# Two-block transformer kernel: VectorE's convolution taps dealt out 3 / 2 / 4 per weight piece instead of 3 throughout

## What is computed

```python
def conformer_conv_branch(a_glu, gate, dw, dw_b, ln_g, ln_b, w_proj):
    a, b = jnp.split(a_glu, 2, axis=-1)
    u = a * jax.nn.sigmoid(b)
    u = lax.conv_general_dilated(
        u, dw[:, None, :], window_strides=(1,), padding=[(CONV_K - 1, 0)],
        dimension_numbers=("NWC", "WIO", "NWC"), feature_group_count=CONV_CH) + dw_b
    u = layer_norm(u, ln_g, ln_b)
...
    return u @ w_proj
```

## Time and profile before

| what | value |
|---|---|
| median of 3 runs | 1293.46 us (1291.17 to 1294.85) |
| the profiled execution, its own time | 1293.89 us |
| its span, first to last instruction | 1292.2 us |
| PE busy | 1134.4 us (88%) |
| DVE busy | 964.9 us (75%) |
| POOL busy | 579.2 us (45%) |
| ACT busy | 567.3 us (44%) |
| mean granted TensorE clock | 0.978 of full speed |

### The profile page before, as it was taken

The page is one execution under the profiler, slowest core; times in us unless marked ns, Lnnn a source line. Parts: engine busy times, 40 slices in busy tenths (PEclk is TensorE's granted clock), DMA queues, the critical chain, the costliest instruction groups (busy, mean ns, idle before and its releaser), DMA issues.

```text
span 1292.2 us, 15750 instructions
## 1 busy us (share of the span) xinstructions
PE 1134.4 (88%) x5652; PEld 785.7 (61%) x5652; DVE 964.9 (75%) x1944; ACT 567.3 (44%) x1036; POOL 579.2 (45%) x576
## 2 busy tenths in 40 slices
PE   6999899999999997999679887798878987777787
PEld 6989798899999996977436332363323632222222
DVE  5589989974578765686798877977679777777554
ACT  5476767664345444695522323413224232222211
POOL 0099999999940000000344544444444444444331
PEclk9999999999999998999889999899998999999999
DMA  7644443444555555535599999999999999999996
GB/s 263 203 132 163 130 131 128 133 135 159 171 193 169 186 163 164 198 103 180 185 421 423 428 427 426 407 426 427 428 426 394 426 427 426 427 426 427 424 428 255
DMA packets 127647, 374.37 MB, mean 290 GB/s; under 512 B 6864, under 2 KB 82640, under 8 KB 94672
## 3 DMA queue, kind: packets, MB, share of 16 engines
q0 software_dynamic: 36864, 268.45, 49.5%
q1 hardware_dynamic: 88496, 100.67, 23.8%
q10 hardware_dynamic: 2208, 4.24, 1.0%
HBM read 372.29 MB, written 1.05 MB: 289 GB/s over the span
## 4 chain that ended last, share of the span: by engine, by line
PE 52%; DMA 23%; DVE 15%; ACT 5%; issue 4%; POOL 0%; SPq 0%; DVEq 0%; POOLq 0%
DMA big<-in_experts,big 17%; PE unit L729 12%; PE unit L418 11%; PE unit L420 11%; PE unit L419 11%; DMA row<-in_experts,big 3%; DVE work L1843 3%; DMA conv_in<-in_experts,big 2%; DVE w_lo L1430 2%; DVE big L1762 1%; DVE conv_acc L1453 1%; ACT L837 1%; DVE big L1759 1%; ACT probs L1178 1%; DVE big L1855 1%
## 5 line engine op out<-in xcount | busy, mean ns | idle before, releaser
L418 PE MATMUL unit<-in_hi,w_hi 128*128 128x256 f32 x1184 | 359.1, 303 | 3.1 <-DVE in_lo L1517 3.1
L419 PE MATMUL unit<-in_lo,w_hi 128*128 128x256 f32 x1184 | 336.2, 284 | 0.0
L420 PE MATMUL unit<-in_hi,w_lo 128*128 128x256 f32 x1184 | 336.2, 284 | 0.0
L1178 ACT ACTIVATE probs<-ident,big 128x128 f32<-128x128 f32 x256 | 102.8, 402 | 447.0 <-DVE big L1855 447.0
L729 PE MATMUL unit<-row,probs 128*128 128x512 f32 x512 | 250.9, 623 | 49.6 <-ACT probs L1178 49.5
L1430 DVE TENSOR_TENSOR w_lo<-w_raw,w_hi 128x2048 fp32r<-128x2048 f32 x91 | 212.0, 2332 | 86.0 <-ACT w_hi L846 86.0
L418 PEld LDWEIGHTS unit<-in_hi,w_hi 128*128 128x128 f32 x1184 | 228.4, 193 | 17.0 <-issue 14.7
L419 PEld LDWEIGHTS unit<-in_lo,w_hi 128*128 128x128 f32 x1184 | 228.4, 193 | 12.2 <-issue 12.0
L729 PE MATMUL unit<-big,probs 128*128 128x512 f32 x384 | 186.7, 617 | 49.9 <-ACT probs L1178 49.9
L420 PEld LDWEIGHTS unit<-in_hi,w_lo 128*128 128x128 f32 x1184 | 228.2, 193 | 0.0
L846 ACT CAST w_hi<-w_raw 128x2048 fp32r<-128x2048 f32 x91 | 172.7, 1903 | 104.9 <-PE unit L420 80.6
(11 more groups left out here) (247 smaller groups left out, 1314.9 us busy)
## 6 DMA issues: line engine op xcount, KB each, us to landing
w_raw<-in_w_in SPq DMA_DIRECT2D x58, 1024.0 KB, 5.1
w_raw<-in_w_mem_kv SPq DMA_DIRECT2D x8, 1024.0 KB, 5.2
w_raw<-in_w_out SPq DMA_DIRECT2D x8, 1024.0 KB, 5.1
w_raw<-in_w_query SPq DMA_DIRECT2D x6, 1024.0 KB, 5.4
w_raw<-in_w_diff_proj SPq DMA_DIRECT2D x4, 1024.0 KB, 5.2
w_raw<-in_w_x_proj SPq DMA_DIRECT2D x4, 1024.0 KB, 5.3
w_raw<-in_w_conv_proj SPq DMA_DIRECT2D x4, 1024.0 KB, 5.2
row<-in_experts,big POOLq DMA_INDIRECT x128
```

The lines of the kernel that those rows point to most:

```text
L418: e.matmul(unit[:, to], *hi_hi, start=first, stop=False)
L419: e.matmul(unit[:, to], *hi_lo, start=False, stop=False)
L420: m = e.matmul(unit[:, to], *lo_hi, start=False, stop=final)
L1178: e.activation(diag_places[g % 12], ident[:, :], ACT.Copy, scale=here).then_inc(*mark("diag", g))
```

## The change

One argument in DVE's loop over `attention`. `ahead` takes it as the number of taps behind each of a slot's two `lo`. It was 3 by default.

```diff
@@ -1920,7 +1920,7 @@
                 if 0 <= n - 12 < X_HEADS:
                     norms.append(partial(cross_probs, n - 12))
-                ahead(s, between=norms)
+                ahead(s, between=norms, convolve=3 if n < 4 else 2 if n < 16 else 4)
                 if n == 0:
                     inverse_rms("mem", mem_tm, lambda half: ("loaded", "mem"))
```

## The result

| | before | after |
|---|---|---|
| median | 1292.22 us (8 runs, 1290.78 to 1294.85) | 1297.91 us (8 runs, 1294.39 to 1299.73) |
| profiled execution, its own time | 1293.89 us | 1297.01 us |
| its span | 1292.2 us | 1295.3 us |
| mean granted clock | 0.978 | 0.982 |

The ratio after to before, over paired runs, is 1.0032 with a 95% interval from 1.0022 to 1.0042: slower by 4.1 us of 1292. The first lies just over the 0.3% that the prediction set as its bound, the second under it.

A forecast was written before the change was run, and what follows sets the result against it. PE, the busiest engine, was taken to wait in the loop for DVE's probabilities, with taps on the path. Terms: -1.7 + 2.7 = +1.0 us, median 1293.46 + 1.0 = 1294.5 us, range 1288.6 to 1298.0.

The forecast's parts named there:

- The lead: PE reaches `conv_mean` 10 us earlier, from 5.8 us of waits for DVE's probabilities and 5.1 us of clock.
- One sign: In the new profile DVE would no longer stand between its `lo` of n = 16 and 17.
- The late taps at no cost: The 21 taps moved later on DVE, in groups of four and nine, cost nothing; 3 us without cover.
- POOL's end as the new gate: Ahead of `conv_mean`, earlier DVE work delays POOL 4.7 us to 375.7; by full durations 5.8 us, to 376.8.
- Rival 1: POOL not delayed, ends at 371.0; `conv_mean` starts 6.4 us earlier; 1289.8 us, or 1287.1 without clock loss; chance 0.13.
- rival 3: Lead at `conv_mean` only 2 to 3 us because ScalarE's roots hold DVE; -2.6 us, 1290.9; chance 0.08.
- rival 4: Change does nothing, as the taps were not what held PE in the loop; 1293.5 us; chance 0.03.
- The price of the wait: PE's 8 us standing ahead of `conv_mean` lowers its clock behind it, costing 1.7 to 3.4, taken as 2.7 us.
- The gain of 1.7 us: `conv_mean` starts at 375.7 instead of 377.4 us; 0.6 us gain by the full durations.
- The slack of 6.4 us: At `conv_mean` before the change: POOL's last instruction ends at 370.96, PE arrives at 377.39 us.
- the likeliest case: POOL's end gates `conv_mean`, with a clock loss of 1 to 4 us; 1291.9 to 1296.9 us; chance 0.66.
- rival 2: Low clock lasts longer behind `conv_mean`, losing 4.3 to 5 us; with 0.6 gain, +4.4 us, 1297.9; chance 0.10.

The follow-up runs named there:

- experiment 1: Changed kernel with the last 8 taps of tile 7 done by DVE instead of POOL: 0.9939 of before, 1287.5 against 1295.51 us.
- experiment 2: Kernel before with the same 8 taps of tile 7 handed from POOL to DVE, three taps per piece kept: 0.9991 of before.
- Experiment 5: Kernel before with two taps per piece only in n = 4 to 7, three elsewhere until used up: 1.0012 of before.
- second and third profile: Both kernels profiled again with no edit; second: before 1.0004, changed 1.0023 of before; third, single executions: 1298.18 us before, 1298.43 us after.
- experiment 4: Changed kernel with 36 unused products on PE ahead of its wait at `conv_mean`: 1.0009 of before.
- second measurement: Changed kernel measured once more with no edit: 1.0023 (1.0012 to 1.0034) of before.
- experiment 3: Changed kernel with 64 unused products on PE ahead of its wait at `conv_mean`: 1.0038 of before.
- experiment 7: Kernel of experiment 1 with one tap per piece in n = 4 and 5: 0.9936 of before.

## Why the prediction came out as it did

**The lead: right.** Forecast were 10 us out of 5.8 us of waits and 5.1 us of clock; measured are 377.39 - 367.29 = 10.1 us, both in the first profile. Over the three profiles of each kernel PE arrives at 375.7 and at 367.4 on average, a lead of 8.3 us. The waits left, 1.37, 0.77 and 0.26 us, were forecast as 1.3, 0.7 and none. The clock in the loop is 1.00. One sign did not come in full: between the `lo` of n = 16 and 17 DVE still stands once, 3.03 us ahead of that of 312.16.

**The late taps at no cost: right.** The nine took 6.60 us, and experiment 1, with all of them, loses nothing.

**POOL's end as the new gate: right.** Forecast 375.7 us, measured 376.17, 376.51 and 376.55. By the Trainium skill, "SBUF — State Buffer", section "SBUF: two separate sides", the estimate was 376.8, with the operations excluding each other for their full length; the measurements lie between the two sums. PE stood 9.0 us where 8 were forecast. Experiments 1 and 2 show the gate. Experiment 5, and the kernel before itself in its second and third profile, show that the end stays there whatever the lead. Rival 1 (POOL not held back), rival 3 (a lead of 2 to 3 us) and rival 4 (taps not on the path) are out.

**The price of the wait: right in size.** 2.7 us forecast, 6.38 - 3.62 = 2.8 us in the first profile, 2.9 and 2.0 in the others; experiment 4 shows it by taking it away.

**The gain of 1.7 us: mis-sized.** This is the term that was off; it measured 0.1 us. It set the new start, 375.7, against the one start of before that I had, 377.39. That was the latest of three: the others are 376.07 and 376.38, so 0.8 us of the 1.7 are the base. The other 0.8 us are POOL's end, which came later than forecast. The slack of 6.4 us, the number which "matters most" by the prediction, belongs to that execution alone; in the other two it is none, since PE already met POOL's later end. Against the mean of the three, 376.6, the changed kernel's start (376.27, 376.61, 376.65, mean 376.5) is a gain of 0.1 us. With it the sum is -0.1 + 2.7 = 2.6 us, 0.20%, inside the interval of the second measurement (0.12 to 0.34) and just under that of the first (0.22 to 0.42). But part of the same price is paid by before: its third profile has a slow `conv_mean` of 5.38 us, which is how the ends come to lie 1.8 us apart.

**What stays open.** From 1.8 us at `conv_mean` to the 3.0 and 4.1 us of the two ratios 1.2 to 2.3 us are left. The six profiles place most of it. On average the changed kernel is 1.8 us behind at the end of `conv_mean`, 2.3 us at its first L658 (586.4 against 584.2), 3.4 us at its first L729, where the expert stage begins (651.4 against 648.0), and 3.0 us at the end of the span. So 1.1 us come between L658 and L729, and they are a fall of the clock at about 600 us: in the first profile of after, L658 to L660 in 599.7 to 604.3 us take 4.57 where they take 3.00 in that of before (597.9 to 600.9). From the first L658 to the last L660 PE takes 48.3 or 48.4 us without the fall and 49.9 to 51.5 us with it; it was met in three of three profiles of after and one of three of before.

Whether it comes goes with the moment at which PE gets there. These are before, the third profile of before, and after (fastest, median and slowest product in ns, then the first and last start in us; the first start is the figure to read):

```profile
L658 PE MATMUL unit<-w_hi,in_hi x32: 389/389/579, 584.5 to 616.8; 128*128 128x512 f32 x32
```

```profile
L658 PE MATMUL unit<-w_hi,in_hi x32: 389/393/774, 585.7 to 621.1; 128*128 128x512 f32 x32
```

```profile
L658 PE MATMUL unit<-w_hi,in_hi x32: 388/390/629, 586.3 to 620.2; 128*128 128x512 f32 x32
```

In the six of the twelve profiles in which this line (L659 or L662 where lines were added) starts at 585.66 us or later, experiments 2 and 3 among them, the clock falls; in the four that start it from 582.28 to 584.53 us, experiments 4 and 5 among them, it doesn't. Of two that come much earlier, experiment 1 at 573.42 us has no fall and experiment 7 at 576.17 us has one. So the fall is not the change's own, but a kernel that comes 2 us later met it more often. Why the moment matters no run shows, and three profiles of each kernel are few.

**The chances.** The forecast was +1.0 us and "same" at 0.77, and the range to 1298.0 held 1297.91 by 0.1 us, which is luck as much as reading. By the prediction's own bound, 1297.4, this median is "slower", which had 0.10; the second measurement would be "same". The mechanism was that of the likeliest case, and rival 2's large clock loss was not what brought the time there.

## What to carry to other kernels

When a wait is taken off the busiest engine, look for the next place where it meets an engine that does not move with it, and work out that engine's end anew: whatever blocks it comes earlier as well, so its slack can be gone at a lead of 2 us. Take such a slack from several profiles, as a clock that falls in some executions and not in others shifts the arrival by more than the term that is being worked out. And gathering short waits into one long wait is not neutral: here one of 9 us cost 2.0 to 2.9 us of clock, while the start behind it came only 0.1 us earlier on average; the cure was to relieve the late engine as well, for 0.6%.

## What the runs showed of the hardware that I had not expected

- POOL's end is a step in the lead: 370.96 us with PE at 377.4; 375.97 and 376.28 with PE at 375.3 and 374.3 (second and third profile of before); 375.24 with PE at 372.5 (experiment 5); 376.17 to 376.55 with PE at 367.3 to 367.5 (the changed kernel). The first 2 us move it by 5, the next 8 us by less than 1.
- The granted clock behind one and the same wait differs between executions: behind the first wait (about 2.1 us) it didn't fall in the first profile of before, and did in the third, where the second wait was then 0.88 instead of 2.26 us.
- A tap on DVE takes 0.52 us with POOL silent (4.13 us for eight) and 0.82 us with POOL in its convolution; the late groups of four and nine took 0.75 and 0.73 us a tap.
